# Four more projections as seven quarter products, with their weight sums made by transfers and VectorE

## The reference

```python
h = rmsnorm(x, norm_g)
a_u, a_v, a_z, b_p, b_z, c_h, c_b, c_c, c_z, gate_logits = split(h @ w_in)      # each part 1024 wide, gate_logits 3 x 1024
ya = spatial_gating(gelu(a_u), gelu(a_v), ...) * silu(a_z)
yb = multiscale_pool(b_p, ...) * silu(b_z)
yc = c_b * causal_depthwise_conv(c_c * c_h, ...) * silu(c_z)
gates = sigmoid(gate_logits)                                                      # three gates
merged = gates[0] * (ya @ w_branch_a) + gates[1] * (yb @ w_branch_b) + gates[2] * (yc @ w_branch_c)
out = rmsnorm(x + merged @ w_out, final_g)
```

## Time and profile before

| | us |
|---|---|
| median of three runs | 1013.89 |
| the profiled execution | 1012.41 |
| its span, first to last instruction | 1010.6 |
| TensorE busy | 998.3 (99%) |
| VectorE busy | 729.7 (72%) |
| ScalarE busy | 579.4 (57%) |
| GpSimd busy | 138.9 (14%) |

### The profile page before, as it was taken

The page is one execution under the profiler, slowest core; times in us unless marked ns, Lnnn a source line. Parts: engine busy times, 40 slices in busy tenths (PEclk is TensorE's granted clock), DMA queues, the critical chain, the costliest instruction groups (busy, mean ns, idle before and its releaser), DMA issues.

```text
span 1010.6 us, 13570 instructions
## 1 busy us (share of the span) xinstructions
PE 998.3 (99%) x5398; PEld 845.0 (84%) x5398; DVE 729.7 (72%) x876; ACT 579.4 (57%) x697; POOL 138.9 (14%) x130
## 2 busy tenths in 40 slices
PE   8999999999999999999999999999999999999997
PEld 8977888888778888888888888888888889999886
DVE  6996889888477667798898757676544657777564
ACT  6437567657377768666767556744544444444533
POOL 4991111101031221110110010100000000000000
PEclk9999999999999999999999999999999999999999
DMA  8863899999774532889999745665464355545531
GB/s 322 256 212 98 277 293 326 335 325 294 212 281 162 198 125 84 292 280 329 298 344 322 282 165 168 237 239 182 150 228 180 125 192 209 183 168 189 198 114 42
DMA packets 35422, 225.23 MB, mean 223 GB/s; under 512 B 4248, under 2 KB 6808, under 8 KB 9504
## 3 DMA queue, kind: packets, MB, share of 16 engines
q1 hardware_dynamic: 24480, 171.45, 45.7%
q0 software_dynamic: 7856, 49.73, 19.4%
q10 hardware_dynamic: 3024, 3.18, 1.2%
HBM read 221.14 MB, written 3.21 MB: 222 GB/s over the span
## 4 chain that ended last, share of the span: by engine, by line
PE 88%; DVE 6%; DMA 3%; ACT 2%; issue 1%; POOL 0%; POOLq 0%; ACTq 0%; DVEq 0%
PE bank L393 56%; PE bank L515 15%; PE bank L379 4%; PE bank L380 4%; PE bank L381 4%; DVE bank L2025 4%; PE bank L429 2%; DMA raw<-in_ws 2%; PE bank L530 1%; PE bank L621 1%; DVE w_lo L1726 1%; PE bank L782 0%; DMA u_scr<-arena 0%; ACT x_hi L1208 0%; ACT w_hi L1181 0%
## 5 line engine op out<-in xcount | busy, mean ns | idle before, releaser
L1726 DVE TENSOR_TENSOR w_lo<-raw,w_hi 128x2048 fp32r<-128x2048 f32 x149 | 342.3, 2305 | 140.2 <-ACT w_hi L1181 139.9
L1181 ACT ACTIVATE w_hi<-raw 128x2048 fp32r<-128x2048 f32 x160 | 305.8, 1913 | 145.5 <-PE bank L393 109.4
L393 PE MATMUL bank<-w_hi,x_hi 128*128 128x512 f32 x544 | 149.6, 397 | 0.2
L393 PE MATMUL bank<-w_lo,x_hi 128*128 128x512 f32 x544 | 145.7, 390 | 0.0
L393 PE MATMUL bank<-w_hi,x_lo 128*128 128x512 f32 x544 | 145.7, 390 | 0.0
L393 PEld LDWEIGHTS bank<-w_hi,x_lo 128*128 128x128 f32 x544 | 102.1, 188 | 21.8
L393 PEld LDWEIGHTS bank<-w_lo,x_hi 128*128 128x128 f32 x544 | 102.1, 188 | 21.5
L393 PEld LDWEIGHTS bank<-w_hi,x_hi 128*128 128x128 f32 x544 | 98.9, 188 | 21.2 <-issue 1.8
L393 PE MATMUL bank<-w_hi,z_hi 128*128 128x512 f32 x320 | 94.3, 394 | 0.4 <-DVE z_lo L1820 0.3
L393 PE MATMUL bank<-w_hi,z_lo 128*128 128x512 f32 x320 | 92.8, 390 | 0.0
L393 PE MATMUL bank<-w_lo,z_hi 128*128 128x512 f32 x320 | 92.8, 389 | 0.0
(11 more groups left out here) (282 smaller groups left out, 1400.5 us busy)
## 6 DMA issues: line engine op xcount, KB each, us to landing
raw<-in_ws SPq DMA_DIRECT2D x160, 1024.0 KB, 5.1
arena<-in_ws POOLq DMA_DIRECT2D x40, 1024.0 KB, 11.4
arena<-u_scr ACTq DMA_DIRECT2D x16, 142.0 KB, 5.0
arena<-in_rows POOLq DMA_DIRECT2D x2, 1024.0 KB, 5.2
toep<-bias_row POOLq DMA_DIRECT2D x1, 1536.0 KB, 45.0
h<-in_x_tok SPq DMA_DIRECT2D x2, 512.0 KB, 4.2
raw<-in_ws SPq DMA_DIRECT2D x2, 512.0 KB, 8.0
arena<-in_rows POOLq DMA_DIRECT2D x2, 512.0 KB, 5.6
```

Of the source, the lines that this page charges most:

```text
L393: ins = pe.matmul(dst, tok(a_part, k, t), w_part[:, s, c], start=first and j == 0 and i == 0, stop=last and j == 2 and i == len(ks) - 1)
L1181: act.activation(w_hi[:, g % SPLIT, :], operand(g), ACT.Copy).then_inc(hi_done, 1)
L1726: dve.tensor_tensor(w_lo[:, g % SPLIT, :], operand(g), w_hi[:, g % SPLIT, :].bitcast(F32), ALU.subtract).then_inc(lo_done, 1)
```

## The change

`STREAM` gives ga, bp, gb and gc six weight operations each (B11, T1, T2, B22, B21, T4), and the projection that follows each of them (wa, bz, wb, wc) five, the second of which is T3. T1 = B11 + B12 and T4 = B12 + B22 are made by GpSimd's transfers (a load, then an accumulating transfer). T2 = T1 + B22 and T3 = T2 + B21 are made by VectorE in the place of T1. There are no areas `sums` in the second block; T1 and T4 lie where something else has lain (`WIDE_SLOTS`), so GpSimd's transfers wait until that is no longer needed. The input sums are made again at the start of the second block, at `av`.

```diff
-PAIRED = (0, 3)
+PAIRED = (0, 3, 5)
+WIDE = {"ga": "wa", "bp": "bz", "gb": "wb", "gc": "wc"}
+WIDE_PARTS = ("B11", "T1", "T2", "B22", "B21", "T4")
+WIDE_SLOTS = {"ga": (10240, 12288), "bp": (6144, 12288), "gb": (2048, 14336), "gc": (6144, 12288)}
...
+            def wide(name, b1, b4, b2, within=None):
+                n, k = wide_no(name), list(WIDE).index(name)
+                product(("p1", n), wide_at(name, "B11"), *of_x(0, t0), b1, True, (S("c_11"), 2 * n - 1))
+                pe.wait_ge(S("q_lo"), 3)
+                product(("p5", n), wide_at(name, "T1"), *of_q(0), b4, True, (S("c_22"), 2 * n - 1))
+                product(("p6", n), wide_at(name, "T2"), *of_q(1), b1, False, (S("c_12"), 2 * n - 1))
+                product(("p3", n), wide_at(name, "B22"), *of_q(2), b4, False, (S("c_12"), 2 * n))
+                if within:
+                    within()
+                product(("p2", n), wide_at(name, "B21"), *of_x(1, t0), b2, True, (S("c_11"), 2 * n))
+                product(("p7", n), wide_at(name, "T4"), *of_q(3), b1, False, (S("c_22"), 2 * n))
...
+                return lambda: product(("p4", n), wide_at(name, "T3"), *of_x(1, t1), b1, False, (S("wide"), 4 * k + 4))
...
-            token_chunk(("gb", 0), G["gb"], x_hi, x_lo)
-            token_chunk(("gb", 1), G["gb"] + 2, x_hi, x_lo, between=y_jobs("yb", au, 0))
-            for n in range(2):
-                token_chunk(("wb", n), G["wb"] + 2 * n, z_hi, z_lo, ready=job_ready("yb") if n == 0 else None,
-                            hooks={(0, 0): [y_jobs("yb", au, 1)]} if n == 0 else {})
+            last = wide("gb", 6, 7, 4, within=y_jobs("yb", au, 0))
+            token_chunk(("wb", 0), chunk_at("wb", 0, 0), z_hi, z_lo, ready=job_ready("yb"),
+                        hooks={(0, 0): [y_jobs("yb", au, 1)], (0, 1): [last]}, second=chunk_at("wb", 0, 1))
+            token_chunk(("wb", 1), chunk_at("wb", 1, 0), z_hi, z_lo)
...
+            lo_ready(pool, wide_at("bp", "T4"))
             pool.dma_start(pool_row, bcast(rows, 3, 2)).then_inc(S("ld_pool"), 16)
             for t in range(TT):
                 for q in range(2):
                     freed(pool, ("mixed", t, q))
+            for w in range(4):
+                freed(pool, ("pool", w))
+            wide_load("gb", "T1")
+            wide_load("gb", "T4")
+            wide_add("gb", "T1")
+            wide_add("gb", "T4")
...
+                feed(o + 2)
+                bank, _ = take(act, ("p1", n))
+                act.activation(w_11, bank[:, :], ACT.Copy).then_inc(S("c_11"), 1)
...
+                feed(o + 8)
+                bank, _ = take(act, ("p4", n))
+                quarter(bank[:, :], 0, 1)
...
+            wide("ga", ACT.Sigmoid, gate, lambda n, t: None, within=lambda: y_hi("ya", 0))
+            y_hi("ya", 1)
...
+            def wide_second(name):
+                lo_ready(dve, wide_at(name, "T1"))
+                o = wide_at(name, "B22")
+                loaded(dve, PIECE_OF[o])
+                a = wide_slot(name, "T2")
+                dve.tensor_tensor(a, a, operand(o), ALU.add).then_inc(S("t2"), 1)
...
+            def wide(name, within=None):
+                n, o = wide_no(name), G[name]
+                feed(o + 3)
+                wide_third(name)
+                feed(o + 5)
...
             for n_ in range(2):
                 c = slice(n_ * 512, (n_ + 1) * 512)
                 for t in range(TT):
                     bank, free = take(dve, ("pooled", n_, t))
                     dve.tensor_tensor(au[:, t, c], bank[:, :], pool_row[:, 0, c], ALU.add).then_inc(free, 1)
+            wide_second("gb")
```

More of the change, by code:

```diff
@@ L76, in ffn_at, with wide_at, chunk_at @@
     return G[f"ffn{layer}"] + FFN_AT[key]
+def wide_at(name, part):
+    return G[WIDE[name]] + 1 if part == "T3" else G[name] + WIDE_PARTS.index(part)
+def chunk_at(name, n, k):
+    return G[name] + ((0, 2, 3, 4) if name in WIDE.values() else (0, 1, 2, 3))[2 * n + k]
+WIDE_SUM = {wide_at(name, part): (name, part) for name in WIDE for part in ("T1", "T2", "T3", "T4")}
 SUM_OF_OP = {ffn_at(layer, p, name): (layer, p, name) for layer in range(2) for p in PAIRS
              for name in ("T1", "T2", "T3", "T4")}
-PIECES = [o for o in range(NOP) if o not in SUM_OF_OP]
+PIECES = [o for o in range(NOP) if o not in SUM_OF_OP and o not in WIDE_SUM]
 NPIECE = len(PIECES)
@@ L946, in _ @@
                                   (S("c_zr"), j + 1) if a else None)
[L947 to L948 removed]
+            last = wide("gc", 4, 5, 6)
             def c_ready(a, t):
                 pe.wait_ge(S("yc_split"), 4 * a + 4)
[L953 to L954 removed]
+            token_chunk(("wc", 0), chunk_at("wc", 0, 0), z_hi, z_lo, ready=c_ready, hooks={(0, 1): [last]},
+                        second=chunk_at("wc", 0, 1))
+            token_chunk(("wc", 1), chunk_at("wc", 1, 0), z_hi, z_lo, between=y_jobs("merged", merged, 0))
             for n in range(2):
@@ L1618, in _ @@
             evac("az", ACT.Silu, az)
-            for n in range(2):
-                ahead(G["ga"] + 2 * n)
-                if n:
-                    for t in range(TT):
-                        plain_hi(("ya", 0, t), z_hi, 0, slice(t * P, (t + 1) * P))
-                ahead(G["ga"] + 2 * n + 1)
-                for t in range(TT):
-                    bank, free = take(act, (("ga", n), t))
-                    act.activation(gate[:, t, n * 512:(n + 1) * 512], bank[:, :], ACT.Sigmoid,
-                                   scale=st2[:, 10 + t:11 + t]).then_inc(free, 1)
@@ L2272, in _ @@
                 if n_:
-                    ahead(G["az"] + 3)
+                    feed(G["ga"] + 1)
+                    wide_second("ga")
                 for t in range(TT):
@@ L2278, in _ @@
                     dve.tensor_tensor(au[:, t, c], au[:, t, c], az[:, t, c], ALU.mult).then_inc(S("ya"), 1)
+            wide("ga", within=lambda: y_lo("ya", 0))
+            y_lo("ya", 1)
             for n_ in range(2):
-                ahead(G["ga"] + 2 + n_)
-                for t in range(TT):
-                    plain_lo(("ya", n_, t), z_hi, z_lo, 4 * n_, slice(t * P, (t + 1) * P))
-            for n_ in range(2):
-                ahead(G["wa"] + 2 * n_ + 1)
+                ahead(chunk_at("wa", n_, 1))
+                if n_:
+                    wide_second("bp")
                 for t in range(TT):
```

264 lines of the change are left out of this document (179 added, 85 removed).

## The result

The changed kernel takes **1029.53 us** (median of 6 runs, 1027.81 to 1031.95). The kernel before, run beside it, takes 1011.64 us. The ratio is 1.0173, with a 95% interval of 1.0148 to 1.0197: slower by 18 us, where 7 were forecast, and outside the range (1009 to 1029). The forecast of 1020.7 stood on 1013.89 for the kernel before, 2.2 us more than was measured beside the changed kernel; so the time is 8.8 us above the forecast, but the change is 11 us larger than it. The profiled execution is 1029.46 us, its span 1027.6 us.

A forecast was written before the change was run, and what follows sets the result against it. TensorE was taken as the bound, busy 998.3 of 1010.6 us. Terms: - 10.9 + 0.2 + 2.2 (ga) + 0 (bp) + 13.1 (gb) + 2.2 (gc) = + 6.8 us on 1013.89, giving 1020.7 us; range 1009 to 1029.

The forecast's parts named there:

- The saving: ga, bp, gb and gc each fall from 96 to 84 matmuls, 48 fewer: 10.9 us off TensorE.
- av: Start of the second block, where the input sums are made: 0.2 us for banks that come free late, 0 to 0.5.
- ga: Before wa's second piece, TensorE stands for the second half of `ya`, converted behind p4's sigmoid: 2.2 us.
- gb: Waits for the late T1 and what hangs on it, plus the second half of `yb`: together 13.1 us.
- R - 790.7 = 10.3: At gb, TensorE's wait for T2's low part, wanted at 806.5 for p6's last third: 10.3 us.
- R: Time gb's T1 lands after load (6.0) and accumulation (10.5): 801.0, earliest 799.5, latest 811.6.
- R + 15.8: At gb, when T2's low part is there, after VectorE's bank readings, T2's sum, eight scalings and products, and conversion.
- the 0.6: At gb, two more waits of 0.4 and 0.2 us, as three conversions and T3's sum run behind each other.
- gc: Two waits in gc: 0.9 us before p6 and 1.3 for VectorE's last low part, together 2.2 us.
- The clock: Rival: behind gb's long gap TensorE returns at 1.2 GHz, 16 matmuls cost 3.4 us more, about 1024; chance 0.15.
- T1 in time would still cost 5.9: At gb, VectorE's own order costs 5.9 us even with T1 before about 794; rival 1013.5 us, chance 0.20.
- the gap before p6: Sign of being right: TensorE's only long gap lies before gb's third quarter product, 6 us or more.

The follow-up runs named there:

- the pair on the kernel before: Kernel before with TensorE made to wait at gb's start until two quarters of y_b are scaled: 1020.2 us; same with 15 small matmuls in the wait: 1017.3 us.
- e_t1early: Changed kernel with T1 and T2 of gb placed in the gate's space, so gb's T1 transfers start some 35 us earlier: 1023.4 us, ratio 1.0109.
- e_gb: Changed kernel with gb's T1 early, T2 made ahead of the four pooled evacuations, low parts of T2 and B22 ahead of the scalings: 1020.7 us, ratio 1.0074.
- e_all: Changed kernel with all corrections: gb's T1 early and work reordered, y ahead of p4, earlier merges in wa, wb, wc, av and gc reordered: 1010.5 us, ratio 0.9981.
- e_yfirst: Changed kernel with ScalarE taking the second half of transposed y ahead of p4's sigmoid at the end of ga and gb: 1030.4 us, ratio 1.0179.

## Why the prediction missed

The direction was right, and so were the kinds of wait that it named. What failed are four terms of the sum: the wait for T1 at gb, sized too small; the lower clock, put at nothing in the sum; the merge in wc, left out; and the preparation in av. Step by step:

- **The saving**, 10.9 us: right. Bp gained its 2.72 us to the hundredth, with no wait, and the cc part is unchanged to 0.01 us.
- **av**, 0.2 us: it was 1.4 in the trace, 1.1 of them one wait. I looked at VectorE's idle time and not at the evacuation of av that now stands behind ScalarE's 1.9 us conversion; with that conversion one evacuation later, 0.7 us came back.
- **ga**, 2.2 us: the wait of 2.15 us released by `z_lo` is there (2.4 with what the chunk loses besides). The slow groups behind it made it 4.0.
- **gb**, 13.1 us: it was 18.3. R - 790.7 = 10.3 was the wait up to p6's last third; it measures 818.37 - (798.40 + 7.25) = 12.7. VectorE's order behind R was right to 0.1 us (R + 15.8 was forecast, R + 15.9 came). What failed is R against TensorE: the load took 5.1 us where 6.0 were put down, the accumulation 13.1 where 10.5 were, and gb started 0.9 us earlier. I had taken a value near the idle end of the earlier trace rows; the middle of that row, 14.3, was nearer. That value rested on a DMA share of about half; while T1 was accumulated the share was 1.02, with the change's own transfers in it, as in the feed-forward parts. The wait at `yb` came as forecast (2.15). The rest, 3.4 us less the 0.6 that it took the place of, is matmuls at the lower clock in p6, p3 and wb.
- **gc**, 2.2 us: its two waits are there (0.85 and 0.9). But the part lost 5.0, since the prediction left out wc: VectorE's merge of the first chunk behind two conversions, 2.4 us (2.6 from start to start). I had stopped counting at the last quarter product.
- **The clock**: forecast as a rival at 3.4 us behind one gap of over 6. It came, as one of the signs of being wrong, in wa, in p5, p6 and p3 of gb and in wb, behind waits of 2.15 us too; the sum had it at nothing. The rival counted 16 slow matmuls behind one gap, a number from no row. On the trace's own chain the slow groups make up 5.0 us of the miss (1.6 in ga's part, 3.4 in gb's). Their price depends on what is late next: 1.6 us where nothing is (the pair on the kernel before, by its parts), and 2.3 us in all in the parts of the changed kernel, where waits for VectorE took back the rest. The medians of the two runs with small matmuls in the changed kernel show no gain.
- **T1 in time would still cost 5.9** in gb, by VectorE's own order: the run with T1 early has 51.64 - (45.45 - 2.72) = 8.9 us above the saving, 6.3 of them waits and some 1.6 slow matmuls, and the best order that I found 4.7. This term, too, was right in kind and small in size, for the merge in wb (0.90 us) and the slow matmuls were not in it.

So the 11 us are, in the trace of the changed kernel: 5.0 of slow matmuls, 2.6 of wc's merge, 2.4 of T1 against TensorE, and 1.2 in av, less some tenths that the forecast had too much. The forecast walked each chain only to its first late operand. The runs showed what stands next: in wa and wb a wait of 2.37 us behind the one of 2.15, in gb one of 2.89 us for the next low part when T2's came in time. By the runs: the orders in wa, wb and wc together are worth 9 us, T1 and gb's order 6 to 9, and both together with the small corrections 19.

Of the signs named, the gap before p6 was 4.8 and not 6 us or more, as 3.2 fell to p5, and it was not the only long one: wc's 2.4 us stood in no sign. TensorE's busy time is shorter by 1.2 us and not by 11, and the slow groups make up 8.6 of the 9.7 between them. The others named as right came true. Of those named as wrong one came, the granted clock under 1.00 behind the gap.

What stays open: why the clock falls behind one wait of 2.37 us in wc and not behind the same wait in another execution; why av starts up to 4 us earlier or later in kernels that are the same up to there; and whether gb in seven products can gain if VectorE's work is moved ahead of it.

## What to carry to other kernels

When fewer matmuls ask for the same number of converted operands, work out what the converting engine has to do in the stretch and hold it against the shorter time of TensorE, all its work and not its average: at gb it was 30.2 of 30.7 us, and the two orders that were tried both left gb to cc at 47.4 us. Walk the chain past the first late operand, to the bank that must be freed for the next chunk: a wait that is taken away uncovers the next one, and two orders may have to change before either shows in the time. A transfer that accumulates should be priced by the middle of its row, not by its idle end, with the DMA share that the change itself brings (0.45 there before, 1.02 while T1 was accumulated), and its target should lie where it is free early, even if a sum must then be written to another place.

## What the runs showed of the hardware

- The granted clock can fall behind waits as short as 2.15 us (wa and wb of the changed kernel), in wa with the first group of four still at full pace and the next two at 1.8 to 1.9 us. The length of the wait does not decide it alone: behind 2.15 us in wb it held in two profiled runs (e_t1early, e_gb), behind 2.37 us in wc it fell in some and not in others, behind 2.89 us in gb it fell in e_gb and not in e_all, and behind 3.46 us before p5 it held in e_yfirst. Behind the waits of 0.9 us in gc no profile shows it fall.
- Small matmuls that nothing reads hold it (1.00 in place of 0.68 in the window behind the wait), at 0.25 us each.
- The accumulating transfer of T1 (1 MB) by GpSimd takes 12.4 to 13.8 us in this block, though the plain load of T1 ahead of it takes 5.1 to 7.4. How much of that is the accumulation and how much the DMA share of 1.02 was not separated. The Trainium skill, page DMA: Bandwidth & Descriptors, section Anatomy of one DMA, has 2.0 us and the bytes at 436 GB/s, an estimate of 4.4 us; the accumulation here is three times that, and the measurement decides.
